# Neighbourhood heads with query tiles of 16 grid columns by 8 rows, and only the key columns in reach

## What is computed

```
def neighbourhood_attention(q, k, v, k_ctx, v_ctx, rpb):
    wr = min(NA_ROWS, rows)                          # 8 of 8 rows
    col_start = np.clip(cols - NA_COLS // 2, 0, GRID_W - NA_COLS)
    col_idx = col_start[:, None] + np.arange(NA_COLS)[None, :]     # 16 columns
    ...
        s_loc = q_r . k_nb * scale + bias            # 8 x 16 neighbours
        s_ctx = q_r . k_ctx * scale                  # 256 context keys
        p = jax.nn.softmax(jnp.concatenate([s_loc, s_ctx]))
        out = p[:nk] . v_nb + p[nk:] . v_ctx
```

## Time and profile before

| | us |
|---|---|
| median of 3 runs | 3384.61 (3384.24 to 3389.86) |
| the profiled execution | 3385.4 |
| its span on the core | 3383.6 |
| busy: TensorE, VectorE, GpSimd, ScalarE | 3318.5, 2178.9, 1844.4, 1100.1 |
| from the end of the input projections to the first product of the output projection | 256 to 435 |
| the neighbourhood units in it | about 332 to 435 |

### The profile page before, as it was taken

How to read it: one execution, slowest core, us unless ns; L and a number is a source line. 1 busy time by engine, 2 the same in 40 slices (tenths; PEclk the granted TensorE clock), 3 DMA queues, 4 the chain that set the end, 5 groups by cost and what they waited for, 6 DMA issues and landing times.

```text
span 3383.6 us, 45712 instructions
## 1 busy us (share of the span) xinstructions
PE 3318.5 (98%) x17148; PEld 2892.6 (85%) x17148; DVE 2178.9 (64%) x4143; ACT 1100.1 (33%) x1507; POOL 1844.4 (55%) x1162
## 2 busy tenths in 40 slices
PE   7999899999999999999999999999999999999998
PEld 4886578888888889999999778888888888999998
DVE  6877720888545224999998340788545324999997
ACT  3226633333344322222223343333334322222222
POOL 0000033377788743877762453377888743877761
PEclk9999999999999999999999999999999999999999
DMA  8777030357988976999995230355669956999995
GB/s 292 267 261 249 26 149 1 128 140 206 238 192 175 190 230 228 372 364 362 385 362 190 75 137 1 114 148 150 145 145 178 180 159 225 368 369 358 362 360 214
DMA packets 542768, 735.38 MB, mean 217 GB/s; under 512 B 243922, under 2 KB 376659, under 8 KB 525908
## 3 DMA queue, kind: packets, MB, share of 16 engines
q1 hardware_dynamic: 386900, 530.65, 48.1%
q0 software_dynamic: 118784, 134.68, 15.6%
q10 hardware_dynamic: 36864, 67.13, 5.5%
HBM read 612.48 MB, written 119.80 MB: 216 GB/s over the span
## 4 chain that ended last, share of the span: by engine, by line
PE 93%; DMA 3%; DVE 2%; ACT 1%; issue 1%; SPq 0%; DVEq 0%; ACTq 0%
PE ps L1430 39%; PE ps L1475 31%; PE ps L1390 5%; PE ps L1225 5%; PE ps L1339 4%; DMA act_scratch<-act_st 2%; PE ps L1253 2%; PE ps L1285 1%; PE ps L1265 1%; PE ps L1450 1%; PE ps L1380 1%; PE ps L1151 1%; DMA modall<-in_w_mod 1%; PE ps L1140 0%; PE ps L1328 0%
## 5 line engine op out<-in xcount | busy, mean ns | idle before, releaser
L1564 POOL DMA_INDIRECT G_scratch<-pick,gidx x512 | 887.8, 1734 | 281.2 <-issue 211.3
L1430 PE MATMUL ps<-xhi,Uhi 128*128 128x512 f32 x2048 | 801.5, 391 | 1.0 <-DVE Ulo L1897 1.0
L1430 PE MATMUL ps<-xhi,Ulo 128*128 128x512 f32 x2048 | 798.1, 390 | 0.0
L1430 PE MATMUL ps<-xlo,Uhi 128*128 128x512 f32 x2048 | 797.5, 389 | 0.0
L1475 PE MATMUL ps<-Hhi,Vhi 128*128 128x384 f32 x2048 | 686.4, 335 | 2.5 <-DVE Hlo L2107 2.5
L1475 PE MATMUL ps<-Hhi,Vlo 128*128 128x384 f32 x2048 | 685.1, 335 | 0.0
L1475 PE MATMUL ps<-Hlo,Vhi 128*128 128x384 f32 x2048 | 685.1, 335 | 0.0
L1897 DVE TENSOR_TENSOR Ulo<-Uraw,Uhi 128x1024 fp32r<-128x1024 f32 x230 | 281.8, 1227 | 579.8 <-ACT Uhi L1015 578.4
L1078 ACT CAST Vhi<-Vraw 128x1024 fp32r<-128x1024 f32 x256 | 269.9, 1054 | 778.3 <-PE ps L1475 763.5
L1571 POOL DMA_INDIRECT picked<-act_scratch,aidx x256 | 373.6, 1459 | 229.3 <-DMA act_scratch<-act_st 151.9
L1037 ACT ACTIVATE act_st<-ps 128x512 f32<-128x512 f32 x256 | 153.2, 598 | 942.2 <-DMA act_scratch<-act_st 607.4
(11 more groups left out here) (293 smaller groups left out, 4026.3 us busy)
## 6 DMA issues: line engine op xcount, KB each, us to landing
Uraw<-in_UT SPq DMA_DIRECT2D x128, 1024.0 KB, 5.8
Vraw<-in_V SPq DMA_DIRECT2D x256, 512.0 KB, 5.7
act_scratch<-act_st ACTq DMA_DIRECT2D x256, 256.0 KB, 2.1
act<-act_scratch SPq DMA_DIRECT2D x256, 192.0 KB
modw<-in_w_mod SPq DMA_DIRECT2D x80, 512.0 KB, 4.7
G_scratch<-zeros SPq DMA_DIRECT2D x32, 1024.0 KB, 10.6
Gin<-G_scratch SPq DMA_DIRECT2D x256, 128.0 KB
ring<-in_query SPq DMA_DIRECT2D x8, 2048.0 KB, 7.8
```

The source lines that it names most:

```text
L1430: mm = nc.tensor.matmul(up_bank(m), w, x[:, k, :], start=(k == 0 and j == 0), stop=(k == KT - 1 and j == 2))
L1564: nc.gpsimd.indirect_dma_start(G_dram[layer].rearrange("m p (t o) -> (m p t) o", o=1), bass.IndirectOffsetOnAxis(ap=gidx[r][:, h * TOPK + ...
```

## The change

- **Token order.** The normalised input of the attention is written with the tokens in column order (token = column * 8 + row) by reading the stream with a stride (`by_row`); the rotation tables are read with a stride too, and `add_projection(0)` puts the result back in row order, reading and writing the stream with a stride.
- **Tiles and reach.** A query tile is now 16 columns by 8 rows. Its queries reach 24 columns (the first and the last tile) or 32 (the two in the middle), so that a neighbourhood unit has 192 or 256 latent keys and 256 context keys for each head, 448 or 512 columns instead of 768. It has 8 blocks to transpose instead of 12. The order of the score products alternates between the two heads, each in a bank of its own.
- **Two banks.** The two pieces of four blocks go through two banks (6 and 5) and both are turned in round u, ahead of the values of u - 1.
- **Mixed values.** Where the reach starts in the middle of a block of 128 tokens, GpSimd builds two mixed value tiles (`vmix`) from halves, once.
- **Tables.** The table is now made of three bands (24, 32 and 24 columns), and since a partition's row offset depends on the query's row, each (row, band, head) is a transfer of its own: 16 partitions x 8 x 24 or 32 elements, 8 x 3 x 2 = 48 transfers for each pair of heads instead of one; 24 more load the mask. They land in a raw buffer of their own (`braw`), so that pairs 2 and 3 may be loaded once `masked_bias` of pairs 0 and 1 is through. `masked_bias` reads the raw table with a stride and writes `btab` in column order, in two or three instructions per part instead of one; part 0 waits for all 48 transfers of its pair (and for pair 0 the 24 of the mask).

The core of the diff:

```diff
...
+BAND = 16
+BANDS = ((0, 24), (8, 40), (24, 56), (40, 64))
+NEAR_W = [(c1 - c0) * NA_ROWS for c0, c1 in BANDS]
+TABLES = (0, 1, 1, 2)
+TABLE_BANDS = (0, 1, 3)
+TABLE_AT = [sum(NEAR_W[j] for j in TABLE_BANDS[:n]) for n in range(len(TABLE_BANDS) + 1)]
+MASK_AT = [at // NA_ROWS for at in TABLE_AT]
+TABLE_PARTS = (((0, 0, 24, 0), (1, 8, 32, 0)), ((1, 0, 8, 24), (2, 8, 24, 0), (2, 0, 8, 16)))
+NEAR_KEYS = (((0, 192),), ((128, 320), (64, 128)), ((256, 448), (192, 256)), ((384, 512), (320, 384)))
+SIDE_AT = (P, P, P, DH)
...
-        btab = [sb(f"btab{n}", at, [P, 2, 16, GRID_W]) for n, at in enumerate((40, 174))]
+        btab = [sb(f"btab{n}", at, [P, 2, TABLE_AT[-1]]) for n, at in enumerate((40, 174))]
+        vmix = [sb(f"vmix{n}", at, [P, CW]) for n, at in enumerate((202, 204))]
+        braw = [sb(f"braw{n}", at, [P, 2, TABLE_AT[-1]]) for n, at in enumerate((45, 168.5))]
...
+        def near_scores(u, c0, c1):
+            b = 3 * (u % 2)
+            return ps[:, b:b + 2, c0:c1]
+        def by_row(x):
+            return x.rearrange("p (r c) -> p c r", r=NA_ROWS)
+        def by_column(x):
+            return x.rearrange("p (c r) -> p c r", r=NA_ROWS)
...
+        def turned(u, n):
+            return ps[:, 6 if n == 0 or units[u][0] == "diff" else 5, :]
...
-            return ((0, 4), (4, KK)) if maps(u) == 1 else ((0, 4), (4, 8), (8, 2 * KK))
+            return ((0, 4), (4, KK)) if maps(u) == 1 else ((0, 4), (4, 8))
+        def keys_of(u):
+            return (NEAR_W[units[u][2]] if maps(u) == 2 else T) + TC
+        def blocks(u):
+            if maps(u) == 1:
+                return [b * P for b in range(KK)]
+            w, side = NEAR_W[units[u][2]], SIDE_AT[units[u][2]]
+            return [m * T + at for m in range(2) for at in (0, side, w, w + P)]
...
-                    sp.wait_ge(bias_used, h - 1)
-                sp.dma_start(btab[h % 2][:, :, :, :], a["btab"][2 * h:2 * h + 2].rearrange("h p s k -> p h s k")
-                             ).then_inc(bias_in[h % 2], 16)
+                    sp.wait_ge(bias_masked, h - 1)
+                if h == 0:
+                    for n, j in enumerate(TABLE_BANDS):
+                        for r in range(NA_ROWS):
+                            sp.dma_start(mask[r:P:NA_ROWS, MASK_AT[n]:MASK_AT[n + 1]],
+                                         a["mask"][j * BAND:(j + 1) * BAND, BANDS[j][0]:BANDS[j][1]]
+                                         ).then_inc(bias_in[0], 16)
+                for r in range(NA_ROWS):
+                    for n, j in enumerate(TABLE_BANDS):
+                        c0, c1 = BANDS[j]
+                        for m in range(2):
+                            sp.dma_start(
+                                braw[h % 2][r:P:NA_ROWS, m, TABLE_AT[n]:TABLE_AT[n + 1]].rearrange(
+                                    "q (s k) -> q s k", s=NA_ROWS),
+                                a["btab"][2 * h + m, j * BAND:(j + 1) * BAND,
+                                          NA_ROWS - 1 - r:2 * NA_ROWS - 1 - r, c0:c1]).then_inc(bias_in[h % 2], 16)
...
+                n = keys_of(u)
+                raw = scores_of(u)[:, m, :] if maps(u) == 1 else near_scores(u, 0, n)[:, m, :]
+                nc.scalar.activation(Ebuf[:, j % 4, 0:n], raw, ACT.Exp, bias=nmx[:, j:j + 1],
...
+                if kind == "near":
+                    w = NEAR_W[qt]
+                    parts, c0 = [], 0
+                    for k0, k1 in NEAR_KEYS[qt] + ((T, TK),):
+                        parts.append((c0, c0 + k1 - k0, k0, k1))
+                        c0 += k1 - k0
+                    for c0, c1, k0, k1 in parts:
+                        for m in range(2):
+                            lo = DH * m
+                            mm = nc.tensor.matmul(near_scores(u, c0, c1)[:, m, :],
+                                                  q[lo:lo + DH, h, qt * P:(qt + 1) * P], kx[lo:lo + DH, h, k0:k1],
+                                                  start=True, stop=True)
+                    mm.then_inc(score_mm, 1)
+                    return
...
-                at_least(pe, probsT_ready, turned_before(u) + n)
-                for b in range(b0, b1):
-                    mm = nc.tensor.transpose(turned[:, (b - b0) * P:(b - b0 + 1) * P],
-                                             Abuf[u % 2][:, b * P:(b + 1) * P], ident[:, :])
+                at_least(pe, probsT_ready, turned_before(u) + n - (1 if u > HEAD_END else 0))
+                for b, at in enumerate(blocks(u)[b0:b1]):
+                    mm = nc.tensor.transpose(turned(u, n)[:, b * P:(b + 1) * P],
+                                             Abuf[u % 2][:, at:at + P], ident[:, :])
...
+                    pe.wait_ge(proj_out, sum(e[0] == "copy" for e in in_evict) + 4)
+                    for n in range(4):
+                        if n == 1:
+                            v, p0, p1 = ((vb[:, 1, :], 0, DH), (vmix[0], 0, P), (vmix[1], 0, P), (vb[:, 2, :], DH, P))[qt]
+                        else:
+                            v, p0, p1 = vb[:, {0: qt, 2: TT, 3: TT + 1}[n], :], 0, P
+                        for m in range(2):
+                            b = 4 * m + n
+                            mm = nc.tensor.matmul(o_bank[m * DH:(m + 1) * DH, :],
+                                                  v[p0:p1, (2 * h + m) * DH:(2 * h + m + 1) * DH],
+                                                  ATbuf[u % 2][p0:p1, b * P:(b + 1) * P],
+                                                  start=(n == 0), stop=(n == 3))
...
+            for n in range(2):
+                nc.gpsimd.tensor_copy(vmix[n][0:DH, :], vb[0:DH, n + 2, :]).then_inc(proj_out, 1)
+                nc.gpsimd.tensor_copy(vmix[n][DH:P, :], vb[DH:P, n, :]).then_inc(proj_out, 1)
...
+                    to, rows, roots_of = dst[:, k, :], src[:, k, :], inv
+                    if n == 0:
+                        to, rows, roots_of = by_column(to), by_row(rows), by_row(inv)
+                    nc.vector.scalar_tensor_tensor(out=to, in0=rows, scalar=scale,
+                                                   in1=roots_of, op0=ALU.mult, op1=ALU.mult).then_inc(x_scaled, 1)
...
-                    dve.wait_ge(bias_in[h % 2], 16 * (h // 2 + 1))
-                table = btab[h % 2][:, :, :, :].rearrange("p h s k -> p (h s) k")[:, 8 * part:8 * (part + 1), :]
-                step(nc.vector.scalar_tensor_tensor(out=table, in0=table, scalar=1.0 / QK_SCALE,
-                                                    in1=mask[:, :].unsqueeze(1).to_broadcast([P, 8, GRID_W]),
-                                                    op0=ALU.mult, op1=ALU.add))
+                    dve.wait_ge(bias_in[h % 2], 16 * NA_ROWS * len(TABLE_BANDS) * (2 * (h // 2 + 1) + 1 - h % 2))
+                if h == 0 and part == 0:
+                    step(nc.vector.tensor_scalar(mask[:, :], mask[:, :], 1.0 / QK_SCALE, None, ALU.mult))
+                for n, c0, c1, to in TABLE_PARTS[part % 2]:
+                    rows = slice(TABLE_AT[n], TABLE_AT[n + 1])
+                    last = nc.vector.scalar_tensor_tensor(
+                        out=by_column(btab[h % 2][:, part // 2, rows])[:, to:to + c1 - c0, :],
+                        in0=by_row(braw[h % 2][:, part // 2, rows])[:, c0:c1, :], scalar=1.0 / QK_SCALE,
+                        in1=mask[:, MASK_AT[n] + c0:MASK_AT[n] + c1].unsqueeze(2).to_broadcast([P, c1 - c0, NA_ROWS]),
+                        op0=ALU.mult, op1=ALU.add)
+                if part < TT - 1:
+                    step(last)
+                else:
+                    last.then_inc(bias_masked, 1)
+                    dve.wait_ge(bias_masked, h + 1)
...
-                    row = NA_ROWS - 1 - 2 * qt
+                    w, at = NEAR_W[qt], TABLE_AT[TABLES[qt]]
+                    step(nc.vector.tensor_reduce(mxc[:, u % 2, :], near_scores(u, w, w + TC), AX, ALU.max))
                     for m in range(2):
-                        near = scores_of(u)[:, m, 0:T]
+                        near = near_scores(u, 0, w)[:, m, :]
                         last = nc.vector.tensor_tensor_reduce(
-                            out=near, in0=near,
-                            in1=btab[h % 2][:, m, row:row + NA_ROWS, :].rearrange("p r c -> p (r c)"),
+                            out=near, in0=near, in1=btab[h % 2][:, m, at:at + w],
...
+                        n = keys_of(u)
+                        last = nc.vector.tensor_scalar(Abuf[u % 2][:, m * T:m * T + n], Ebuf[:, (j + m) % 4, 0:n],
...
+                    sums, rows = ps[:, f, :], hT[:, f, :]
+                    if layer == 0:
+                        sums, rows = by_column(sums), by_row(rows)
+                    nc.vector.scalar_tensor_tensor(out=rows, in0=sums, scalar=mods[:, layer, g1 + f, 0:1], in1=rows,
...
```

61 lines of the change are left out of this document (25 added, 36 removed).

## The result

| | us |
|---|---|
| before, median of 4 runs beside the change | 3384.4 (3384.1 to 3389.9) |
| after, median of 4 runs | 3443.6 (3439.5 to 3452.1) |
| ratio, 95% interval | 1.0167 (1.0155 to 1.0179) |
| span of the profiled execution, before and after | 3383.6 and 3440.5 |

The change is slower by 59 us. The forecast was 3395, 10 us slower, with a range of 3372 to 3424: the direction was right, the size wrong by a factor of six.

What follows compares the result with a forecast made beforehand. TensorE bound the units (5.10 of 5.85 us); after the change SyncE's queue of small loads decides. Stage +6.5, low clock +1.5, strides +2 make +10.0 on 3385.4; with the median 0.8 lower, 3395 us, range 3372 to 3424.

Steps and rivals of the forecast that it cites:

- the price of an issue: SyncE's queue: each small table or mask load takes 0.48 us to issue, with 0.42 and 0.65 as the ends.
- the queue is dearer: Rival on SyncE's queue: many short pieces fill it, each load costs 0.65 us, +33, 3428 us; chance 0.12.
- the three signs of being wrong: Issues under 0.40 or over 0.55 us, zeros not holding the queue for 38 us, units not falling below 4 us.
- the zeros at the pace of the data: 16 zero writes on SyncE's queue behind pair 1: two accepted at once, 14 at 2.634 us, together 38.1 us.
- the wait in front of pair 2: VectorE reaches pair 2's part 0 in round 18 and waits some 33 us for all 48 transfers, stopping the core.
- the four rounds until pair 3's part 0 ... about 17 us: VectorE between the masks of pairs 2 and 3: 4 x 3.46 us and two normalisations, less than the queue's 23.
- the tail of 39: From pair 3's masking to the output projection's first product: nine units with the drain, 39 us, bounds 36 and 47.
- the +2 for strides: Strided operands, mainly in `add_projection(0)`'s stream reads and writes, cost 2 us more, bounds 0 and 8.
- The units: Neighbourhood units: TensorE 3.3 us, VectorE 3.46 and binding, so a unit falls from 5.85 to 3.46 us.
- the second bank: Neighbourhood units: removes the 0.75 us a unit in which one bank must be emptied before it is filled again.
- strides double on VectorE too: Rival: `scaled(0)`, masks and projection's add cost +8 instead of +2, VectorE's unit 4.0, 3406 us; chance 0.07.
- The tables in time: Rival: tables land in time, VectorE paces the stage, 38 us saved, 3350 us; chance 0.13 together with a partial gain.

Runs made afterwards that it cites:

- The probe: Kernel with one table load per pair, plus six waves of small transfers behind pair 3's tables; issues to 16 partitions took 0.59 to 0.60 us.
- e_one_bank: Kernel with one table load per pair, both turned pieces sent through one bank instead of two: ratio 0.9976 to the kernel before, first output product at 423.8.

## Why the prediction was wrong

**The failed step is the price of an issue.** "I take 0.48 (nearest in size and in an idle queue)". It is 0.645 with its gap (0.60 + 0.045), 0.67 with the few long ones. The rival "the queue is dearer" had the number, 0.65, for a reason that doesn't hold: the queue was not full. The probe shows it: 16 such loads into an idle queue cost 0.599 each. I had read size and idleness as what mattered. The earlier trace rows are loads to all 128 partitions; the one row with the right price, I set aside as a full queue's. It isn't of the right shape either (`sublg` has one number in each of 128 partitions), so the rows allowed a price between 0.42 and 0.65 with none to choose by, and over 216 issues the ends of that span are 50 us apart. Of the three signs of being wrong that the prediction names, this one came, issues over 0.55; the zeros did hold the queue for 38.3 us and the units did fall below 4. From the stage's start to pair 3's mask, against the forecast:

| term | forecast | measured |
|---|---|---|
| start of the queue's work | 255.7 | 259.4 |
| mask, 24 issues | 11.5 | 15.1 |
| pairs 0 and 1, 96 issues | 46.1 | 64.6 |
| zeros | 38.1 | 38.3 |
| pairs 2 and 3, 96 issues | 49.5 | 64.8 |
| landing of the last load | 2.0 | 1.5 |
| pair 3 masked | 402.9 | 443.9 |

37.4 of the 41 us are the issues, 3.7 the later start. The later start I put down to the strides ahead of the stage; fewer strides give back 2.6 of it. The order of the queue, the zeros at the pace of the data, the wait in front of pair 2 and a second one were as described. That the wait is 53 and not 33 us, and that pair 1 is waited for too (73.7 in three waits), follows mostly from the same number. The step "the four rounds until pair 3's part 0 ... about 17 us" was short: 23.2 with one load. It cost nothing here, since the queue needed 32.

**The rival of the dear queue was itself too low**, 3428: it charged 0.17 for each issue but kept the tail of 39 and the +2 for strides. The measured time is 16 us above it.

**The tail.** Forecast 39, measured 44.0, within its bounds. With one load it is 41.8, with fewer strides 39.2 (403.04 - 363.87). The 2.2 us between the first two stand with the low clock: 0.59 for 6 us behind the second wait, where it is 1.00 with one load, and 0.50 from 481 us on, where the last transposes take 1.97 us instead of 1.09. The next 2.6 are about 1.0 of strides (the last two `Abuf` start 33.5 and 32.4 us behind pair 3's mask) and 1.6 of clock again: 0.62 in the last 5.9 us with one load, 1.00 with fewer strides. That the last version meets the forecast of 39 is in part luck, since in all three the last two `Abuf` take 2.40 us instead of 0.82, beside four products of GpSimd into `ring_lo` (475.50 to 480.59 in the change). The forecast had no such term; in the kernel before, two `Abuf` beside the same products take 1.40 instead of 1.15.

**The units.** TensorE's 3.42 was forecast as 3.3, VectorE's 3.53 as 3.46, and 5.85 became just that where nothing else stands between. This part was right for the units themselves, and the second bank, which the forecast booked as 0.75 us a unit, is worth 11 us (e_one_bank), near the 12 us that 16 units make. Over the nine last units the tail still comes to 4.9 us each, with the normalisations and the drain.

**The strides.** "I take +2 (bounds 0 and 8)": up to 3.7 ahead of the stage, about 1 in the tail, and behind the projection hT's adds, 2.89 for three and 1.10 for the fourth in the chain against 2.81 for four, +1.2. About 6, inside the bounds and well above the 2; for `xm`, with two strided reads in SBUF, the rival "strides double on VectorE too" was nearer the truth (1356 ns against 747). The ScalarE row was the right kind of evidence, and I priced it down without a row. The sentence of the Trainium skill that I set beside this term (VectorE: DVE Perf Modes, section "Mode 1× (REGULAR) — the baseline") says that odd strides work, not that they cost nothing; the 0 was mine.

**The tables in time** (3350) was the first rival. Made true by one load it is 3366 us with the strides, and 0.991, 3354 us, with most of them gone: some 30 of its 38 us are there.

## To carry to other kernels

A layout that multiplies the number of transfers is paid on the issuing queue, here at one price per transfer from 1.5 to 32 KB. Count the issues between two things that the core waits for, and take the price from transfers like yours; where no row has them, let the dearest row count as much as the nearest. If a table can be laid out as the tile wants it, one load beats longer pieces, half as many transfers and a second queue for half of them (first output product at 412.8 against 483.9, 429.5 and 445.7). Before a helper engine takes over work, look whether it stops the engine that it is to relieve.

## What the runs showed of the hardware

- An issue on SyncE's queue cost 0.59 to 0.60 us to 16 partitions of any arrangement tried, 0.43 to 128 partitions with one piece of 96 bytes each, 0.64 to 128 partitions with eight such pieces (two transfers). Number of partitions and pieces don't settle it: other loads to 128 partitions with one row each took 0.43 (`ident`), 0.58 (`mask` with one load) and 0.60 (`rot`), and one with eight rows each 0.37 (`ring`). GpSimd's queue issued the same small transfers in 0.52 us, beside SyncE's.
- Strided fp32 operands in SBUF cost VectorE, for 512 elements: 747 ns without, 1121 with one strided write, 1356 with two strided reads, 1125 with a strided read and write of the same tile; rope's product 682 and 1069 with one strided read. A strided read from PSUM cost nothing: hT's add takes 750 ns with it and 751 in the kernel before. The Trainium skill (Advanced Engine Details and Errata, section "Memory Cachelines") says that SBUF pays a penalty when each access falls on another line of 16 bytes; the first rows agree, at strides of 32 and 256 bytes. It says that any non-contiguous pattern in PSUM slows matmuls; for VectorE the row of 750 ns shows no such cost.
- While GpSimd ran its scaling pass over SBUF, a TENSOR_SCALAR of VectorE between two SBUF tiles stood still until it ended, 2.93 us instead of 0.17, whereas a reduction of 1536 elements from PSUM, begun 1.3 us ahead of the pass and still running 0.5 us into it, took its usual 1.76. Beside GpSimd's table additions (345.94 to 349.54) a reduction and an addition on PSUM ran at their usual 0.69 and 0.43 us. The Trainium skill (SBUF — State Buffer, section "Who interferes with whom") says that the one that comes second blocks fully when VectorE is in a two-port mode; these rows agree, though none shows the mode.
